# Seven places for expert weights instead of six, one of them under x1, which is kept in memory meanwhile

## The reference

```python
x = x + concat(z_a, z_b) @ W_out                    # x1 in the kernel
t = rmsnorm(x, g_ffn)
grp = argmax(t @ w_coarse + b_coarse)               # one of 4 groups for each row
top_v, top_i = top_k(fine logits of that group, 2)  # two of its 8 experts
for e in range(32):
    hid = silu(t @ w_gate[e]) * (t @ w_up[e])       # 1024 -> 256
    out += combine[:, e] * (hid @ w_down[e])        # 256 -> 1024
y = rmsnorm(x + out, g_final)
```

## Time and profile before

| | |
|---|---|
| median of three runs | 564.33 us (563.63 to 565.37) |
| the profiled execution | 564.4 us |
| its span in the trace | 562.6 us |
| PE busy / DVE / ACT / POOL | 87% / 44% / 18% / 34% |
| moved by DMA | 141.17 MB, mean 251 GB/s |
| first rows of the experts' blocks on PE | 272.4 us |
| first product with expert weights | 276.0 us |
| last product with `w_down` ends | 533.5 us |
| `y` rows: first load issued | 537.5 us |

### The profile page before, as it was taken

How to read it: one execution, slowest core, us unless ns; L and a number is a source line. 1 busy time by engine, 2 the same in 40 slices (tenths; PEclk the granted TensorE clock), 3 DMA queues, 4 the chain that set the end, 5 groups by cost and what they waited for, 6 DMA issues and landing times.

```text
span 562.6 us, 9132 instructions
## 1 busy us (share of the span) xinstructions
PE 492.2 (87%) x3423; PEld 294.9 (52%) x3424; DVE 246.5 (44%) x496; ACT 100.5 (18%) x204; POOL 190.1 (34%) x283
## 2 busy tenths in 40 slices
PE   6999999999999999996689889897869687488992
PEld 3787777777776455553344444443434343244430
DVE  4139999999955112347222222222112212022237
ACT  5131111011125332334011101111001101011123
POOL 2013818837678001112233233332313313033101
PEclk9999999999999999997799999999979989599997
DMA  8993016000002991139588999999999999998077
GB/s 330 320 398 73 0 32 268 2 0 1 1 1 96 371 406 42 40 131 399 175 337 276 371 367 408 395 394 392 385 388 395 382 398 387 399 402 333 31 277 235
DMA packets 35504, 141.17 MB, mean 251 GB/s; under 512 B 10322, under 2 KB 10338, under 8 KB 23193
## 3 DMA queue, kind: packets, MB, share of 16 engines
q1 hardware_dynamic: 29194, 127.91, 60.1%
q0 software_dynamic: 4960, 9.45, 5.1%
q10 hardware_dynamic: 1327, 3.49, 1.6%
HBM read 134.47 MB, written 13.17 MB: 262 GB/s over the span
## 4 chain that ended last, share of the span: by engine, by line
PE 66%; DMA 17%; issue 6%; SPq 4%; DVE 4%; ACT 2%; POOL 1%; POOLq 0%; DVEq 0%; ACTq 0%
PE bank L1222 25%; DMA region_w<-in_w_up 11%; PE bank L1305 9%; PE bank L1418 8%; PE bank L1438 7%; PE bank L1413 7%; DMA region_w<-in_w_in 3%; SPq L388 3%; DMA slot<-y_rows 2%; PE bank L1215 2%; PE bank L1404 2%; PE bank L1366 1%; PE bank L1331 1%; PE bank L1428 1%; DVE ua L1107 1%
## 5 line engine op out<-in xcount | busy, mean ns | idle before, releaser
L1222 PE MATMUL bank<-region_h,region_w 128*128 128x256 f32 (+1 forms) x576 | 140.6, 406 | 0.0
L1222 PEld LDWEIGHTS bank<-region_h,region_w 128*128 128x128 f32 x576 | 109.2, 190 | 29.8
L1107 DVE TENSOR_TENSOR ua<-ua,bank 128x128 f32<-128x128 f32 x30 | 8.7, 289 | 184.1 <-ACT ua L619 184.1
L1418 PE MATMUL bank<-region_w,z 128*32 128x256 f32 x512 | 48.7, 431 | 14.8 <-DMA region_w<-in_w_up 11.3
L1305 PE MATMUL bank<-region_w,z 128*128 128x512 f32 x128 | 56.7, 596 | 0.2 <-ACT z L564 0.2
L1438 PE MATMUL bank<-region_w,ua 128*32 128x512 f32 x344 | 51.9, 598 | 0.0
L770 POOL COPY gcol<-gidx 64x1 uint32 (+1 forms) x30 | 5.4, 179 | 137.4 <-DVE sb_rows L1098 137.4
L905 DVE SCALAR_TENSOR_TENSOR z<-ub,par,z 128x512 f32<-128x512 f32 x60 | 47.5, 792 | 0.0
L905 DVE SCALAR_TENSOR_TENSOR region_x<-ub,par,region_x 128x512 f32<-128x512 f32 x56 | 46.6, 832 | 0.0
L701 POOL TENSOR_TENSOR ub<-region_x 128x512 f32<-128x512 f32 x4 | 25.3, 6335 | 58.5 <-ACT ub L518 31.9
L1305 PEld LDWEIGHTS bank<-region_w,z 128*128 128x128 f32 x128 | 23.8, 190 | 28.0 <-issue 26.3
(11 more groups left out here) (230 smaller groups left out, 655.5 us busy)
## 6 DMA issues: line engine op xcount, KB each, us to landing
region_w<-in_w_down SPq DMA_DIRECT2D x21, 1024.0 KB, 17.4
region_w<-in_w_gate SPq DMA_DIRECT2D x16, 1024.0 KB, 14.9
region_w<-in_w_up SPq DMA_DIRECT2D x16, 1024.0 KB, 17.2
region_w<-in_w_in SPq DMA_DIRECT2D x4, 2048.0 KB, 19.0
slot<-in_w_gate SPq DMA_DIRECT2D x6, 1024.0 KB, 14.9
slot<-in_w_up SPq DMA_DIRECT2D x6, 1024.0 KB, 14.6
slot<-in_w_down SPq DMA_DIRECT2D x6, 1024.0 KB, 15.8
region_x<-in_w_up SPq DMA_DIRECT2D x5, 1024.0 KB, 24.7
```

The source lines that it names most:

```text
L1222: ins = mm(ps[2 * bank + j][:, 0:LEN[j]], sec[name][:, k, c * P:(c + 1) * P], hT[:, k, CUT[j]], start=(k == 0), stop=(k == KC - 1))
L1418: ins = mm(ps[1][r0:r0 + H, 0:2 * P].rearrange("p (w f) -> p w f", w=2), xT[:, k, half * H:(half + 1) * H], wgu[i][:, :, k, h, :], start=( ...
```

## The change

There are seven places. The new one (index 6, `LAST`) lies in `RH`, where `x1` is: gate, up and the first half of down; the second half of down lies in `ub`. SP therefore stores each tile of `x1` to memory (`x1_rows`), loads expert 6 there before its loop, and loads `x1` back once all blocks of experts 0 to 27 are done; the readers of `x1` at the end wait for that (`s_x1r`). Expert e now lies in place e modulo 7. SP's loop holds seven reloads and runs three times, with four more behind it. Since pairs and seven places have no common period below 14, PE's loop holds seven bodies and runs twice, with one body ahead of it (experts 0, 1) and one behind (30, 31): nine bodies. The three entries of `bound` for the first pair are read ahead of the wait for its rows. SP now waits for both first gathers before the gate part of 5.

```diff
-NSLOT = 6
+NSLOT = 7
...
-        slot_gu = [reg[:, lo:lo + 2 * PART] for reg, lo, _, _ in places]
+        LAST = NSLOT - 1
+        slot_gu = [reg[:, lo:lo + 2 * PART] for reg, lo, _, _ in places] + [RH[:, 0:2 * PART]]
         slot_dn = [reg[:, lo:lo + PART] for _, _, reg, lo in places]
+        last_dn = [RH[:, 2 * PART:2 * PART + D], ub_t[:, 0:D]]
...
             def load_part(i, part, e):
+                src = parts[part][:, bass.ds(e, 1), :].rearrange("p e n -> p (e n)")
+                if (i, part) == (LAST, 2):
+                    for c, dst in enumerate(last_dn):
+                        sp.dma_start(dst, src[:, c * D:(c + 1) * D]).then_inc(s_wexp[i][part], 16)
+                    return
...
+            def store_x1(t):
+                sp.wait_ge(s_x1, 2 * t + 2)
+                sp.dma_start(x1_dram[t * P:t * P + TROWS[t], :], x1[0:TROWS[t], t, :]).then_inc(s_x1d, 16)
+
+            for t in range(NT - 1):
+                store_x1(t)
             sp.wait_ge(s_o, NT)
             load_expert(3, 3)
+            store_x1(NT - 1)
...
-            sp.wait_ge(s_gath[0], 16)
+            for i in range(2):
+                sp.wait_ge(s_gath[i], 16)
             load_part(5, 0, 5)
+            sp.wait_ge(s_x1d, 16 * NT)
+            load_expert(LAST, LAST)
             sp.wait_ge(s_tab, 1)
...
             for i in range(NE % NSLOT):
                 reload(NE // NSLOT, i)
+            used = sp.value_load(bound[0:1, NE // NSLOT * NSLOT:NE // NSLOT * NSLOT + 1], min_val=1, max_val=NBLK)
+            sp.wait_ge(s_down, used)
+            for t in range(NT):
+                sp.dma_start(x1[0:TROWS[t], t, :], x1_dram[t * P:t * P + TROWS[t], :]).then_inc(s_x1r, 16)
...
             dve.wait_ge(s_gfin, 16)
+            dve.wait_ge(s_x1r, 16 * NT)
...
             keep_busy(24)
             pe.wait_ge(s_tab, 1)
+            first_pair = blocks_of(0)
             pe.wait_ge(s_mv, 1)
             tokens(0, KC).then_inc(s_xt_ps, 1)
...
-            with pe.Fori(0, NE // NSLOT) as it:
-                for i in range(0, NSLOT, 2):
-                    pair(it, i)
-            for i in range(0, NE % NSLOT, 2):
-                pair(NE // NSLOT, i)
+            pair(0, (0, 1), (0, 0), first_pair)
+            with pe.Fori(0, 2) as it:
+                for e in range(2, 2 + 2 * NSLOT, 2):
+                    pair(it * (2 * NSLOT) + e, (e % NSLOT, (e + 1) % NSLOT),
+                         (it * 2 + e // NSLOT, it * 2 + (e + 1) // NSLOT))
+            pair(NE - 2, ((NE - 2) % NSLOT, (NE - 1) % NSLOT), (NE // NSLOT, NE // NSLOT))
+            pe.wait_ge(s_x1r, 16 * NT)
             pe.wait_ge(s_diag, 2 * len(BY_PE))
```

More of the change, by code:

```diff
@@ L1399, in _, with down_rows @@
             wdn = [w.rearrange("p (c d) -> p c d", c=F // P) for w in slot_dn]
+            def down_rows(i, c, h):
+                if i == LAST:
+                    return last_dn[c][:, h * 512:(h + 1) * 512]
+                return wdn[i][:, c, h * 512:(h + 1) * 512]
             H = T // 2
@@ L1432, in block_of @@
                 pe.wait_ge(s_yc, g + 1)
-                for i in sorted(set(halves)):
-                    pe.wait_ge(s_wexp[i][2], turn * 16 + 16)
+                for half in range(1 if halves[0] == halves[1] else 2):
+                    i, turn = halves[half], turns[half]
+                    pe.wait_ge(s_wexp[i][2], turn * 32 + 32 if i == LAST else turn * 16 + 16)
                 for c in range(F // P):
@@ L1438, in block_of, with blocks_of @@
                         ins = mm(ps[3][quarter * H:(quarter + 1) * H, :], hidT[:, c * T + r0:c * T + r0 + H],
-                                 wdn[halves[quarter % 2]][:, c, h * 512:(h + 1) * 512],
+                                 down_rows(halves[quarter % 2], c, h),
                                  start=(c == 0), stop=(c == F // P - 1))
                 ins.then_inc(s_down, 1)
+            def blocks_of(e):
+                return (pe.value_load(bound[0:1, bass.ds(e, 1)], min_val=0, max_val=NBLK - 1),
+                        pe.value_load(bound[0:1, bass.ds(e + 1, 1)], min_val=1, max_val=NBLK),
+                        pe.value_load(bound[0:1, bass.ds(e + 2, 1)], min_val=1, max_val=NBLK))
@@ L1443, in _, with pair @@
             keep_busy(24)
             pe.wait_ge(s_tab, 1)
+            first_pair = blocks_of(0)
             pe.wait_ge(s_mv, 1)
             tokens(0, KC).then_inc(s_xt_ps, 1)
[L1448 to L1452, removed]
+            def pair(e, slots, turns, ends=None):
+                first, after, end = ends or blocks_of(e)
+                i, j = slots
@@ L1454, in pair @@
                 for part in range(2):
-                    pe.wait_ge(s_wexp[i][part], it * 16 + 16)
+                    pe.wait_ge(s_wexp[i][part], turns[0] * 16 + 16)
                 with pe.If(after > first + 1):
                     with pe.Fori(first, after - 1) as g:
-                        block_of(g, (i, i), it)
+                        block_of(g, (i, i), (turns[0], turns[0]))
                 for part in range(2):
-                    pe.wait_ge(s_wexp[i + 1][part], it * 16 + 16)
-                block_of(after - 1, (i, i + 1), it)
+                    pe.wait_ge(s_wexp[j][part], turns[1] * 16 + 16)
```

10 lines of the change are left out of this document (6 added, 4 removed).

## The result

| | before | after |
|---|---|---|
| median of 4 runs each, us | 563.98 (563.08 to 565.37) | 572.18 (570.25 to 577.59) |
| ratio, 95% interval | 1 | 1.0161 (1.0122 to 1.0201) |
| profiled execution, its span, us | 564.4, 562.6 | 577.59, 575.8 |
| instruction packets in the whole run | 16 | 39 |

The change made the kernel 1.6% slower, 8.2 us, where 8.7 us of gain had been forecast. The profiled execution is the slowest of its four runs, 5.4 us over their median, so sums taken from it are larger than the 8.2 us. Expert 3's load is issued at 254.1 us in it where it stood at 250.99. That belongs to the execution: in kernels whose first half is the old one, the same load is issued at 249.49 (e2_six_big) or 253.46 (pad56). By the first product only 0.7 us of the 3.1 are left, since the gap in front of it is 1.75 us shorter and some 0.6 are made up on the way.

The account below looks back on a forecast made before the run. The prediction took the saturated weight stream, which makes PE wait for expert 27, as the bound. Its terms, -8.1 - 1.5 + 0.3 + 0.6 = -8.7 us, gave 555.7 us, range 552.5 to 559, chance 0.66.

Parts of the forecast that it names:

- What bounds the kernel: Expert stage: the weight stream saturates DMA from 312 to 515 us, and PE waits for expert 27's weights until 486.19.
- Part 1: Before the loop: expert 6 loaded from about 272 us, so the saturated stretch holds one expert less; -8.1 us.
- part 2: Near 304 us: the DMA pipe no longer runs dry between experts 7 and 8; -1.5 us, bounds 0 to -4.1.
- near tie: Kernel's end: expert 31's `w_up` lands at 518.1, pair (30, 31) starts at 519.25; both expected to move with the stream.
- Part 3: Before the first matmul: `bound` loads moved ahead of the wait for rows; 1.4 us earlier, no direct worth at the end.
- Part 4: x1's store may delay the last h2 rows or first gather, +0.3 us (0 to +0.7); its reload stays hidden.
- Part 5: PE's longer loop: some 20 more instruction packets take DMA time; +0.6 us (0 to 0.9), no stall counted for PE.
- These 12 us hide the miss: 0: Return to the loop's head near 400 us: a fetch of 2.5 to 7.9 us, covered by PE's lead before expert 27.
- The clock: After the long wait PE's first block stays slow, 6.15 against 3.68 us; slow blocks behind the two earlier waits go away.
- Fetch stalls, slower: Rival: in the loop's second pass each code packet costs PE a landing, 2.5 us or more; +14, 578 us; chance 0.11.
- break-even of 1.7 us a packet: Within the slower rival: about 5 packets behind pair (26, 27), unhidden, cancel the 8.7 us gain at this price each.

Follow-up runs that it names:

- e2_six_big: The kernel before with only PE's code laid out longer: a loop of six pair bodies run twice, four bodies behind it; 571.5 us, ratio 1.0142.
- pad56: The kernel before with 56 never-executed matmuls behind a false condition, three times in each loop body; 688.38 us, ratio 1.2194.
- held24: The kernel before plus a place under x1 holding only expert 24; PE's loop of three bodies runs four times, four bodies behind; 560.8 us, ratio 0.9933.
- x1_six: The changed kernel with six places and the old loop; x1 still stored and read back, its place left empty; 566.54 us, ratio 1.003 to the kernel before.
- e1_unroll7: The changed kernel with PE's loop written out as sixteen bodies in a row, no return; 564.38 us, ratio 1.0 to the kernel before.
- light_after: The changed kernel with reloads of only 128 of 2048 numbers a row; 552.56 us, against 544.0 for the kernel before with the same light reloads.

## Why the prediction was wrong

- **What bounds the kernel: right for before.** The weight stream bound it from 396 us on. held24 has one expert less to load in that stretch and starts (26, 27) 9.7 us sooner than the earlier trace rows, 8.8 counted from the first product.
- **Part 1 and part 2, one expert earlier and no dry spell: right in size, not all of it kept.** The forecast for the start of (26, 27) was near 477.5; held24 has 476.53. The near tie that the earlier trace rows showed then took 3 us, in a wait for expert 31 and a slow block behind it; the forecast had let both move together. The median gain of held24 is 3.2 us, its profiled one 6.4 (564.4 - 558.02). So even with the short loop the time stays some 5 us above the forecast of 555.7, and 3 of them are this wait and this block.
- **Part 3, the loads of `bound`: right.** The gap before the first product is 0.88 us in the changed kernel, 2.63 before; 1.75 less where 1.4 was taken.
- **Part 4, x1: hidden as said, its price not shown to be wrong.** The way back is issued at 513.33 us and the readers follow at 544.48; no wait of PE names it. Timeline of SP of the kernel after:

```profile
513.33 3.21 SPq L478 DMA_DIRECT2D region_h<-x_rows  x5
```

  The round trip with the second gather's wait measures 1.7 us (0.2 to 3.2) where 0.3 was taken (x1_six).
- **Part 5, code: the step that failed.** Its count was good: 23 packets more where about 20 were said, and 21 of them in 330 to 520 us. Its prices were not. "These 12 us hide the miss: 0" rested on a miss of at most 7.9 us, taken from the gathers, and on PE being that far ahead. The miss was 11.45, longer than any gather's landing; in a nearly empty pipe it was still 6.74. Two packets start within the 11.45 us, where one landing was taken. Behind it two more gaps, of 4.32 and 4.88 us, had no term. And "a fetch in sequence costs PE nothing I can see" was read from the first pass of a short loop, where the pipe was not yet full. From the first product to the start of (26, 27) PE took 220.9 us instead of 210.2. Since 19.3 us of weight waits went, about 30 us of its own time came, 24 of them in issue gaps. PE reached the pair at 497.64 us, where the forecast had PE there at 465.7 and the weights at 477.4: 32 us late, of which the 12 of cover took their part and 20 became time. With the return alone taken away (e1_unroll7) 7.8 us come back.
- **The clock: no net loss.** The forecast counted on slow blocks going away with the waits. The three blocks behind the stalls take 16.2 us (5.64, 5.46, 5.12) where 3.87 each would be 11.6; but the kernel before has three such blocks behind its three waits, with 18.1 us. The third is the 6.15 of the earlier trace rows; the other two, before (columns as above, clock 0.57 and 0.69):

```profile
413.86:420.30 6.44, 6.44 (x66) 3.29 (x67) 0.00 (x0) 0.00 (x0) 0.00 (x0) 0.57 1.02 384
450.12:455.59 5.47, 5.47 (x66) 3.26 (x67) 0.00 (x0) 0.00 (x0) 0.00 (x0) 0.69 1.02 357
```

- **The rivals.** "Fetch stalls, slower" held the mechanism and named the place. It priced a packet at 2.5 us and got 578; the median is 572.2. Its break-even of 1.7 us a packet over the five packets behind (26, 27) was not how it went: behind that pair PE took 46.8 us against 47.3, no loss at all (its first block is 1.0 us less slow than before, so 0.5 us of own time came). The loss stood ahead of it. Against that rival I had put rows that show a loop which fits; no row could speak for one that doesn't, and 0.11 was too little for a case that the trace could not exclude.

## What to carry to other kernels

A loop has a footprint in code as well as in data. Where a change makes an engine's loop longer, count its instruction packets, and if the loop no longer stays, put the fetch at the return on the path with its full price: here 7 to 11 us, and the clock behind it. A rotation can often be lengthened by using the extra place once, ahead of or behind a short loop (held24), instead of by rotating through it. And when an edit is costed at nothing because a wait covers it, add up everything that will use that same cover.

## What the runs showed of the hardware

- PE's loop of some 5 to 7 instruction packets of 16 KB stays; one of some 10 is fetched again each round, at about 2.5 us a packet with jumps in it (pad56).
- One return to code that is gone: 6.74 us in a nearly empty pipe, 11.45 in a full one; to code that is there, 1.78.
- New code walked through in sequence: some 1.5 us for six packets more in a nearly empty pipe (light_after); in a full pipe gaps of up to 4.2 us (e1_unroll7) and 4.9 (the changed kernel, before (26, 27)), but not always (0.85 in held24). What decides between these wasn't tried. A candidate: in this data the pairs (12, 13), (14, 15) and (16, 17) have one block each, so PE jumps over two of the three block codes of a body and uses up code fastest there. Both gaps of e1_unroll7, the two of e2_six_big and the one before (18, 19) of the changed kernel stand right behind such a pair.
- A slow fetch is not a slow transfer: a packet takes 1.1 us in the full pipe and 1.2 in the nearly empty one, the returns 11.45 and 6.74.
- A jump forward over 56 matmuls that never run costs 3.0 us at the first pass (pad56, 5.64 against 2.63).
- The three stalls of the changed kernel each left the next block at 5.1 to 5.6 us in place of 3.9 (granted clock 0.66, 0.69 and 0.74 over these blocks). That comes on top of the stall and is in no wait.
